# A mixture of experts on one core: the experts' lists and results go through device memory, and ScalarE requests ten of each expert's weight units

## What is computed

```
def moe_swiglu(u, w_router, b_router, w_gu, w_down):
    logits = (u @ w_router).astype(F32) + b_router.astype(F32)
    top_val, top_idx = lax.top_k(logits, TOP_K)                 # 2 of 8 experts for each of 256 tokens
    weights = jax.nn.softmax(top_val, axis=-1)
    combine = jnp.einsum('...k,...ke->...e', weights, jax.nn.one_hot(top_idx, N_EXPERTS, dtype=F32))
    out = jnp.zeros(u.shape[:-1] + (w_down.shape[-1],), F32)
    for e in range(N_EXPERTS):
        out = out + combine[..., e:e + 1] * swiglu(u, w_gu[e], w_down[e]).astype(F32)
    return out.astype(u.dtype)
```

## Time and profile before

| | us |
|---|---|
| median of 3 runs (1954.95, 1956.15, 1963.43) | 1956.15 |
| span of the profiled execution, first to last instruction | 1955.1 |
| start of the experts' products | 1144 |
| start of the last matmul on weights | 1935 |
| PE busy over the span | 1830.6 |
| DVE busy over the span | 1401.0 |
| ACT busy over the span | 1046.3 |

### The profile page before, as it was taken

How to read it: one execution, slowest core, us unless ns; L and a number is a source line. 1 busy time by engine, 2 the same in 40 slices (tenths; PEclk the granted TensorE clock), 3 DMA queues, 4 the chain that set the end, 5 groups by cost and what they waited for, 6 DMA issues and landing times. The chain is left out here.

```text
span 1955.1 us, 24303 instructions
## 1 busy us (share of the span) xinstructions
PE 1830.6 (94%) x9018; PEld 1506.6 (77%) x9018; DVE 1401.0 (72%) x1513; ACT 1046.3 (54%) x1277; POOL 107.2 (5%) x101
## 2 busy tenths in 40 slices
PE   7999998899999996999987779999999999999996
PEld 2688676687887875887976568888888888888885
DVE  4675358655555565775576569898989898988887
ACT  2543354532222235323334557777777777777775
POOL 2251120000000000000012000000000000000000
PEclk9999898899999998999999779999999999999998
DMA  7543102444333553444300359999999999999996
GB/s 263 173 166 115 44 1 76 140 158 154 130 129 131 165 178 119 147 138 146 130 1 23 139 176 350 352 350 355 347 345 354 350 353 351 352 352 350 351 353 245
DMA packets 142914, 418.07 MB, mean 214 GB/s; under 512 B 7754, under 2 KB 30450, under 8 KB 142717
## 3 DMA queue, kind: packets, MB, share of 16 engines
q1 hardware_dynamic: 141496, 417.02, 59.9%
q10 hardware_dynamic: 1350, 0.11, 0.1%
HBM read 416.06 MB, written 1.05 MB: 213 GB/s over the span
## 5 line engine op out<-in xcount | busy, mean ns | idle before, releaser
L2717 DVE TENSOR_TENSOR w_low<-e_ring,w_high 128x1536 fp32r<-128x1536 f32 (+1 forms) x387 | 617.2, 1620 | 88.2 <-ACT w_high L2636 88.2
L2636 ACT ACTIVATE w_high<-e_ring 128x1536 fp32r<-128x1536 f32 (+1 forms) x385 | 524.6, 1381 | 177.9 <-PE ps L2550 174.3
L2548 PE MATMUL ps<-w_high,list_h 128*128 128x512 f32 (+1 forms) x768 | 291.6, 380 | 4.2 <-DVE list_l L2736 4.2
L2550 PE MATMUL ps<-w_high,list_l 128*128 128x512 f32 (+1 forms) x768 | 287.1, 374 | 0.0
L2549 PE MATMUL ps<-w_low,list_h 128*128 128x512 f32 (+1 forms) x768 | 286.7, 373 | 0.0
L1694 ACT ACTIVATE fw_high<-ring 128x1024 fp32r<-128x1024 f32 x62 | 65.7, 1060 | 261.7 <-PE ps L1623 189.8
L1745 DVE TENSOR_TENSOR fw_low<-ring,fw_high 128x1024 fp32r<-128x1024 f32 x62 | 75.9, 1224 | 148.6 <-ACT fw_high L1694 148.6
L2548 PEld LDWEIGHTS ps<-w_high,list_h 128*128 128x128 f32 x768 | 144.8, 189 | 25.4 <-issue 4.6
L2550 PEld LDWEIGHTS ps<-w_high,list_l 128*128 128x128 f32 x768 | 144.6, 188 | 21.5
L2549 PEld LDWEIGHTS ps<-w_low,list_h 128*128 128x128 f32 x768 | 145.0, 189 | 20.7
L1621 PE MATMUL ps<-u_high,fw_high 128*128 128x512 f32 x352 | 140.6, 399 | 7.9 <-DVE fw_low L1745 7.9
(11 more groups left out here) (419 smaller groups left out, 3453.5 us busy)
## 6 DMA issues: line engine op xcount, KB each, us to landing
e_ring<-in_e_w_gu_dram SPq DMA_DIRECT2D x99, 1536.0 KB, 8.5
e_ring<-in_e_w_down_dram SPq DMA_DIRECT2D x48, 1536.0 KB, 8.6
bg_area<-in_mod_w_dram SPq DMA_DIRECT2D x72, 512.0 KB, 4.3
e_ring<-in_e_w_gu_dram SPq DMA_DIRECT2D x33, 1024.0 KB, 7.4
ring<-in_f_w_gu_dram SPq DMA_DIRECT2D x22, 1024.0 KB, 7.7
ring<-in_h_w_in_dram SPq DMA_DIRECT2D x10, 2048.0 KB, 8.5
e_ring<-in_e_w_down_dram SPq DMA_DIRECT2D x16, 1024.0 KB, 7.0
ring<-in_m_w_in_dram SPq DMA_DIRECT2D x6, 2048.0 KB, 8.9
```

The costliest lines, as they stand in the source:

```text
L2548: nc.tensor.matmul(out, high[:, f, :], w_high[:, c, :], start=(f == 0), stop=False)
L2550: last = nc.tensor.matmul(out, low[:, f, :], w_high[:, c, :], start=False, stop=(f == total - 1))
L2636: nc.scalar.activation(piece(k.w_high, p), raw_piece(k, p), ACT.Copy).then_inc(S.high_done, 1)
L2717: nc.vector.tensor_tensor(piece(k.w_low, p), raw_piece(k, p), piece(k.w_high, p).bitcast(F32), ALU.subtract).then_inc(S.low_done, 1)
```

## The change

- **Rows through device memory.** A tensor `expert_rows` of 18 blocks of 128 rows of 4 KB is added in device memory. SP fills it with zeros (one transfer of 9.4 MB) in `mlstm_heads`, from rows that POOL clears.
- **Lists.** At the start of `experts` POOL works out in small operations, for each token and rank, the number of its row, and writes the token rows there with four indirect transfers (512 KB each). Each later list is then loaded by SP in one transfer (`load_list`, behind the request of unit 8), in the place of gather and copy; PE turns it at p = 24 as before. The first list is still gathered by PE.
- **Results.** ACT copies an expert's result out of PSUM in two halves (`keep_y`, at p = 46 and 47), unweighted and not split; SP stores it in the list's own block (`store_y`, 512 KB, behind the request of the next expert's unit 6). After the last store POOL fetches each token's two results with four indirect transfers, and `finish` weighs and adds them on DVE.
- **Removed from every expert:** `scatter`, `turn_places`, `gather` (but the first), `list_rows` (but the first), the copies of the places, `y_high`, `y_low`, `find`, `add`.
- **Requests.** Units 5, 7, ... 23 (ten) are requested by ACT, at p = 1, 5, 9, ... 37, behind its split of piece p + 4 (and the SiLU of p); SP requests the other 14.
- `finish` loads ACT's table for the square root ahead, and handles the two tiles of tokens one behind the other on DVE.

```diff
@@ mlstm_heads
+        @block.sync
+        def _(sp):
+            sp.wait_ge(zeros_made, 1)
+            sp.dma_start(k.lists.rearrange("b p n -> p b n"),
+                         k.zero_rows.unsqueeze(1).to_broadcast([P, LIST_BLOCKS, D])).then_inc(lists_zeroed, 16)
+            sp.wait_ge(lists_zeroed, 16)
@@ experts
+    BY_SCALAR = range(E_RING + 1, E_UNITS, 2)
...
+            def store_y(it):
+                kept = sp.snap(it * 2 + 2)
+                sp.wait_ge(S.y_kept, kept)
+                sp.nop()
+                sp.dma_start(k.lists[it], k.y_rows[:, :]).then_inc(S.y_stored, 16)
+
+            def load_list(it):
+                sp.wait_ge(S.listed, 64)
+                sp.nop()
+                turned = sp.snap(it + 1)
+                sp.wait_ge(S.list_turned, turned)
+                sp.nop()
+                sp.dma_start(k.list_rows, k.lists[it + 2]).then_inc(S.rows_in, 16)
...
                 for j in range(E_RING, E_UNITS + E_RING):
-                    need = sp.snap(it * PIECES + (2 * j + 2))
-                    sp.wait_ge(S.low_done, need)
-                    load_expert_unit(k, sp, e if j < E_UNITS else following, j % E_UNITS)
+                    if j not in BY_SCALAR:
+                        need = sp.snap(it * PIECES + (2 * j + 2))
+                        sp.wait_ge(S.low_done, need)
+                        load_expert_unit(k, sp, e if j < E_UNITS else following, j % E_UNITS)
+                    if j == E_RING + 2:
+                        store_y(it)
+                    if j == E_RING + 4:
+                        load_list(it)
...
+            for rank in range(2):
+                for i in range(2):
+                    row = bass.IndirectOffsetOnAxis(ap=k.row_no[:, rank, i:i + 1], axis=0)
+                    pool.indirect_dma_start(k.lists.rearrange("b p n -> (b p) n"), row, k.tok[:, 2 + i, :], None).then_inc(S.listed, 16)
+            n = passes(pool)
+            stored = pool.snap(n * (16 * EXPERTS) + 16)
+            pool.wait_ge(S.y_stored, stored)
...
+                    pool.indirect_dma_start(k.tok[:, 2 * rank + i, :], None, k.lists.rearrange("b p n -> (b p) n"),
+                                            row).then_inc(k.y_back[rank, i], 16)
...
                     def follow(p):
-                        if p == 3:
-                            scatter(ys + 1, adds, 0)
-                        elif p == 8:
-                            scatter(ys + 2, adds + 2, 1)
-                        elif p == 12:
-                            turn_places(it, adds, e)
-                        elif p == 20:
-
-                            gather(it + 1)
-                        elif p == 24:
+                        if p == 24:
+                            pe.wait_ge(S.y_kept, it * 2 + 2)
+                            pe.wait_ge(S.rows_in, it * 16 + 16)
                             turn_list(it + 1)
...
+            def keep_y(it, half):
+
+                act.wait_ge(S.used, it * PIECES + (E_BUFS + PIECES - 1 + half))
+                if half == 0:
+                    act.wait_ge(S.y_stored, it * 16 + 16)
+                nc.scalar.activation(k.y_rows[:, half * HALF:(half + 1) * HALF], k.ps[:, 4 + half, :], ACT.Copy).then_inc(S.y_kept, 1)
...
                     for p in range(PIECES):
+                        if p >= PIECES - 2:
+                            keep_y(it, p - (PIECES - 2))
                         split(it, p + E_BUFS)
                         if tile_of(p) and tile_of(p)[1] == 0:
                             silu(it, tile_of(p)[0], p)
...
+                        if p % 2 and E_RING + (p + 1) // 2 in BY_SCALAR:
+                            j = E_RING + (p + 1) // 2
+                            need = act.snap(it * PIECES + (2 * j + 2))
+                            act.wait_ge(S.low_done, need)
+                            load_expert_unit(k, act, e, j)
@@ finish
+            nc.scalar.activation(k.rms[:, 2:3], k.eps[:, 0:1], ACT.Sqrt)
...
             for i in range(2):
+                dve.wait_ge(k.y_back[0, i], 16)
+                nc.vector.tensor_scalar(k.acc[:, i, :], k.acc[:, i, :], weight[0][:, i, :], None, ALU.mult).then_inc(weighed, 1)
+                dve.wait_ge(weighed, i + 1)
+                dve.wait_ge(k.y_back[1, i], 16)
+                nc.vector.scalar_tensor_tensor(out=k.acc[:, i, :], in0=k.tok[:, 2 + i, :], scalar=weight[1][:, i, :],
+                                               in1=k.acc[:, i, :], op0=ALU.mult, op1=ALU.add).then_inc(joined, 1)
```

More of the change, by code:

```diff
@@ L2327, in routing @@
     r = k.route
-    L, EQ, CAND, OH1, OH2, L2, COMB, SEL = (r[:, n, :, :] for n in range(8))
+    L, EQ, CAND, OH1, OH2, L2, _, SEL = (r[:, n, :, :] for n in range(8))
     V1, V2, IDX, W1, W2, EX = (r[:, 8 + n // 4, :, 2 * (n % 4):2 * (n % 4) + 1] for n in range(6))
@@ L2551, in three_passes @@
                 last.then_inc(S.used, 1)
[L2553 to L2571, removed]
             def turn_hidden(it, t):
@@ L2584, in turn_hidden @@
                 last.then_inc(S.hturned, 1)
-            gather(0)
+            gather_first()
+            pe.wait_ge(S.rows_copied, 2)
             turn_list(0)
@@ L2680, in _ @@
                     it = ps_ * EXPERTS + e
-                    for half in range(2):
-                        y_high(it * PIECES, half)
                     for p in range(PIECES):
+                        if p >= PIECES - 2:
+                            keep_y(it, p - (PIECES - 2))
                         split(it, p + E_BUFS)
@@ L2703, in _ @@
                             list_high(it + 1)
-            for half in range(2):
-                y_high(n * (EXPERTS * PIECES), half)
         @block.vector
@@ L2745, in hidden @@
                                         k.ps[:, 2 * (t % 2) + 1, 0:n], ALU.mult).then_inc(S.hid_done, 1)
[L2747 to L2759 removed]
+            find_first()
             for p in range(1, E_BUFS):
@@ L2767, in _ @@
                     it = ps_ * EXPERTS + e
-                    ys, adds = 2 * it, 4 * it
-                    for half in range(2):
-                        y_low(ys + 1 + half, half)
                     for p in range(PIECES):
@@ L2793, in _ @@
                             list_low(it + 1)
-            for half in range(2):
-                y_low(n * (2 * EXPERTS) + (1 + half), half)
-            for half in range(2):
-                add(n * (4 * EXPERTS) + 2 * half, half)
 def finish(k):
@@ L2803, in finish @@
     squared, root, gated, scaled, added, stored = (k.sem("out_" + n) for n in ("squared", "root", "gated", "scaled", "added", "stored"))
+    weighed, joined = k.sem("out_weighed"), k.sem("out_joined")
+    weight = [k.route[:, 8 + n // 4, :, 2 * (n % 4):2 * (n % 4) + 1] for n in (3, 4)]
     with nc.Block() as block:
```

115 lines of the change are left out of this document (47 added, 68 removed).

## The result

The changed kernel takes **1940.1 us**, median of five runs (1939.0 to 1948.7); before it was 1956.2. The ratio is 0.9916, 95% interval 0.9895 to 0.9937. The forecast was 1939.0, its range 1922 to 1960. The profiled execution took 1940.06 us, with a span of 1938.3.

A forecast was written before the change was run, and what follows sets the result against it. PE was taken to set the pace at 98.63 us per expert, with the transfers just keeping up. From 1956.15 us, eight experts save 21.6 and the end adds 4.5: 1939 us, range 1922 to 1960.

The forecast's parts named there:

- What leaves PE: Per expert, gather, two scatters and the turn of places leave PE: 4.27 us, from 98.63 to a floor of 94.36.
- DVE and ACT: Per expert, DVE loses 4.2 us and ACT ends at 77 to 80 us of 94.4; DVE does not become the bound.
- The transfers' floor: Per expert, weights plus store and list need 90.0 to 97.5 us; PE briefly runs out; 95.9 us taken, 2.7 less.
- Ten requests on ACT: Per expert, ACT's weight requests go out late, 20 us in sum; priced within the 1.5 us above PE's floor.
- Zeroing: Filling 9.4 MB with zeros in `mlstm_heads` takes 27 us where nothing is moved: costs nothing.
- SP's queue: Result store and list load on SP's queue in each expert wait for nothing and cost only their bytes.
- The tail: After the last expert, store, four indirect reads and DVE's weighing and adding: +4.5 us, bounds +0.7 and +9.5.
- The sum: Whole kernel: 1956.15 - 21.6 for eight experts + 4.5 at the end = 1939 us.
- PE goes on setting the pace: Rival for the experts: transfers average 378 GB/s and PE still binds; 1926 us, chance 0.22.
- The late requests from ACT: Rival for the experts: a third of 20 us lateness reaches PE, 101.1 us per expert, 1980 us in all; chance 0.10.
- Their border: Lateness from which ACT's late requests decide the outcome: 4.3 us per expert, 0.43 us per request.

The follow-up runs named there:

- experiment 6: Changed kernel with all units from 5 to 23 requested by ACT (19 and not 10): 1938.2 us, ratio 0.9896.
- experiment 9: Changed kernel with ACT's request placed ahead of its split of piece p + 4 and of the SiLU, not behind: 1943.0 us, ratio 0.9922.
- experiment 10: Changed kernel with ACT's ten units in pairs (6 and 7, 10 and 11, up to 22 and 23), not every second unit: 1942.5 us, ratio 0.9914.
- experiment 2: Changed kernel with the list's load requested behind unit 12 (not 8) and the result's store behind unit 20 (not 6): 1940.5 us, ratio 0.9902.

## Why the prediction came out

**The number is right, and one of its two causes is wrong; that it came within 1 us is in part luck.**

*What leaves PE*: right. PE's floor was put at 94.36 us from the starts of gather, scatters and turn; with all requests by SP it is 94.21.

*DVE and ACT*: right. DVE's 33.6 us were 32.3, ACT's 11.2 were 14.3, and neither became the bound.

*The transfers' floor*: the value is right, 95.9 forecast against 95.89 and, in the other execution, 95.07. The reason fails, and of the places named for the stalls, pieces 3 to 12, piece 9 has 2.7 us and piece 18, outside them, 4.7. The step said that PE would run out because 378 GB/s on average is too much for a stage that had moved between 294 and 396. With one queue the same bytes flow at 380 GB/s and PE never waits. A middle between two bounds had been taken for lack of a nearer row; the 352 GB/s of the earlier trace rows were what PE asked for, not what the transfers could give. The trace gives 408 GB/s over 20 us of zeroing. The Trainium skill's lower figure (DMA: Bandwidth & Descriptors, "Where 436 GB/s comes from"), about 358 GB/s, does not bind here, with 380 over 700 us; its 425 for one core alone is not contradicted, and not reached in the 408 of the zeroing.

*Ten requests on ACT*: this is the step that failed. It put every request one ACTIVATE late, 1.5 us, and two of them 4 us, since it took ACT to request only when its ACTIVATE was done. The timeline of the changed kernel around unit 7, as the earlier trace rows:

```profile
1347.31 1.49 ACT L2659 ACTIVATE w_high<-e_ring 128x1536 fp32r<-128x1536 f32 x1 [0.30 <-DMA e_ring<-in_e_w_gu_dram]
1348.82 1.28 ACT L2683 ACT_TABLE_LOAD   x1
1348.96 0.38 ACTq L2451 DMA_DIRECT2D e_ring<-in_e_w_gu_dram  x1
...
1351.98 0.59 ACT L2683 ACTIVATE resid<-ps 128x512 f32<-128x512 f32 x1
```

The request, which stands behind the split of p + 4 and the second SiLU in the program, goes out at 1348.96, 3 us before that SiLU starts, and 1.65 us before the split of p + 4, at 1350.61. Over seven experts ACT's requests came 0.49 us behind the split that frees the slot, SP's 0.15. The 20 us of lateness were 5 in all. And yet the queue cost all of PE's stalls, 6 to 12 us in the stage: not by being late, for the greater part, but by being a second one. Experiments 6, 9 and 10 say so; how the 6 to 12 us divide exactly stays open. The prediction had the sentence for it, from the Trainium skill ("Issuing engines are not separate DMA queues", same page), that requests of several engines share the DMA engines and interleave; unit 9 agrees with it (11.5 us to land against 10.05). It was left without a price.

*Zeroing* and *SP's queue*: right in that nothing waited for them. But store and load, priced by their bytes alone, lie beside unit 9, which lands 7.6 us after its request once they are moved (experiment 2) and not 11.5.

*The tail*: mis-sized. +4.5 forecast, bounds +0.7 and +9.5; it measured +9.2, and +10.1, outside the bounds, in the second execution. The store was as forecast: it landed at 1915.2, 4.7 us after the copy (4.1 forecast) and 1.3 behind the last prefetch. The reads were not: issued every 1.25 us (1 forecast), they took 4.3 to 5.3 us to land and not 2.7, so that the last stood 9.9 us behind the store and not 6.7. And the prediction had DVE begin with the first tile; the end of the block held it until the last read had landed.

*The sum*: -21.6 + 4.5 was -23.7 + 9.2 in the profiled execution. The stage gave 2.1 more than forecast, as the first expert gained 4.4 us, and the tail took 4.7 more; that the total is right to 1 us is helped by a start 2.3 us early, which belongs to the execution and not to the change. In the second execution it is -29.4 in the stage, +10.1 in the tail and +2.6 at the start, which sums to the same: in both, a stage that gained more than forecast paid for a tail that cost more. That the two errors cancel is luck.

*The rivals*: "PE goes on setting the pace" (0.22) is what one queue gives: 94.21 us per expert. The late requests from ACT that would have made it slower did not come. Their border was also set wrong: 4.3 us per expert is where PE's saving is used up; with the tail of 4.5 and the half percent it is 4.9, 0.49 us per request.

## What to carry to other kernels

Try to fill a ring of buffers that just keeps up from one queue, in the order of use. Here the second queue took nothing off SP that mattered, and it let a later unit take rate from the one that was needed first. A rate in a trace may be only what was asked for, as the 352 GB/s were here; look whether the consumer waits for it before you call it a limit. POOL's indirect reads, used by the next stage, held the end of the block here until all had landed; issuing them in the next stage took that wait away and gave back 1.3 us of it.

## What the runs showed that was not expected

- ACT's transfer requests passed ahead of work that stands before them in its program: they went out beside a running ACTIVATE or table load, 0.49 us on average behind the split it waited for.
- POOL's drain at the end of the experts' block lasted 8.2 us, until its indirect transfers had landed.
- An indirect read of 128 rows of 4 KB took POOL 0.95 us and 0.3 to the next. The first of four landed after 4.3 us, the others after 5.3.
- Two executions of one kernel had equal times, 1940.06 us, with stages of 766.8 and 761.1 us and starts 5 us apart.
- Unit 9 was held up on SP's queue while unit 10, asked 4 us later on ACT's, landed 1.7 us before its use (experiment 10).
